# Block products in four column groups of TensorE, and the convolution's norm spread over the last two blocks of the projection

## What is computed

```python
h = rmsnorm(x, norm_mix)
z = h @ w_in                       # 256 x 6104 columns
u_glu, q_nsa, kv_nsa, g_nsa, c_q, c_kv, k_rope, g_merge = split(z)

# the convolution: 31 taps per channel, then a layer norm over 512 channels
a, b = split(u_glu); u = a * sigmoid(b)
u = depthwise_conv(u, conv_w) + conv_b
y_conv = silu(layernorm(u, ln_g, ln_b)) @ w_branch_conv

# the compressed attention's blocks: 15 overlapping windows of 32 rows, 2 groups, 64 channels
blk = tok[:, idx] + pos            # 30 rows (15 windows x 2 groups) of 32 * 64 = 2048
k_cmp = gelu(blk @ w1_k + b1_k) @ w2_k       # w1: 2048 x 256, once for keys, once for values
v_cmp = gelu(blk @ w1_v + b1_v) @ w2_v
```

## Time and profile before

| | before |
|---|---|
| median of 3 runs | 2211.2 us (2202.96 to 2211.48) |
| the profiled execution | 2208.97 us, span 2207.5 us |
| TensorE busy | 2122.1 us, 96% |
| VectorE busy | 1365.1 us, 62% |
| ScalarE busy | 1127.2 us, 51% |
| mean granted TensorE clock | 0.985 |

### The profile page before, as it was taken

One profiled execution on the slowest core, in us unless ns is written; L12 is line 12 of the kernel. 1 busy time (PEld: TensorE's weight loads), 2 busy tenths in 40 slices (PEclk: granted clock), 3 DMA queues, 4 the chain that ended last, 5 costly groups with the idle time before them and its releaser, 6 DMA issues.

```text
span 2207.5 us, 25418 instructions
## 1 busy us (share of the span) xinstructions
PE 2122.1 (96%) x9936; PEld 1736.3 (79%) x9936; DVE 1365.1 (62%) x1948; ACT 1127.2 (51%) x1818; POOL 72.0 (3%) x106
## 2 busy tenths in 40 slices
PE   8999899999999989999999999979999999999998
PEld 6877787888887778788788877658788788877887
DVE  5977655554797665555465447665655655577553
ACT  5547455443555546544454446534544544377442
POOL 0000100000000200000000000100000000010000
PEclk9999999999999999999999999989999999999999
DMA  6562353555555234345455544313555555544453
GB/s 236 193 216 89 121 181 122 189 187 177 189 191 191 80 131 154 139 184 191 172 189 184 190 181 172 129 43 115 193 181 189 190 183 189 190 177 165 178 187 133
DMA packets 52950, 369.27 MB, mean 167 GB/s; under 512 B 6207, under 2 KB 6463, under 8 KB 9312
## 3 DMA queue, kind: packets, MB, share of 16 engines
q1 hardware_dynamic: 49104, 356.54, 44.7%
q10 hardware_dynamic: 3216, 9.53, 1.4%
q0 software_dynamic: 512, 1.57, 0.4%
HBM read 366.31 MB, written 1.31 MB: 167 GB/s over the span
## 4 chain that ended last, share of the span: by engine, by line
PE 86%; DVE 6%; ACT 5%; issue 1%; DMA 0%; POOL 0%; ACTq 0%; DVEq 0%
PE ps L481 25%; PE ps L483 25%; PE ps L482 25%; PE ps L569 2%; DVE nT_lo L1243 2%; PE ps L620 1%; DVE ring_lo L1181 1%; PE ps L742 1%; PE ps L553 1%; PE ps L604 1%; ACT nT_hi L1975 1%; ACT upper_w L1911 1%; ACT ostage L1963 1%; PE ps L821 1%; PE ps L539 1%
## 5 line engine op out<-in xcount | busy, mean ns | idle before, releaser
L482 PE MATMUL ps<-ring_lo,nT_hi 128*128 128x512 f32 x1952 | 764.2, 392 | 0.0
L1181 DVE TENSOR_TENSOR ring_lo<-ring,upper_w 128x1024 fp32r<-128x1024 f32 x443 | 536.1, 1231 | 279.7 <-ACT upper_w L1911 276.9
L1911 ACT CAST upper_w<-ring 128x1024 fp32r<-128x1024 f32 x443 | 456.2, 1056 | 340.7 <-PE ps L483 170.8
L481 PE MATMUL ps<-upper_w,nT_hi 128*128 128x512 f32 (+1 forms) x1352 | 540.5, 400 | 19.0 <-DVE ring_lo L1181 11.5
L483 PE MATMUL ps<-upper_w,nT_lo 128*128 128x512 f32 (+1 forms) x1224 | 478.8, 391 | 0.0
L482 PEld LDWEIGHTS ps<-ring_lo,nT_hi 128*128 128x128 f32 x1952 | 370.9, 190 | 73.3 <-issue 0.5
L481 PEld LDWEIGHTS ps<-upper_w,nT_hi 128*128 128x128 f32 x1352 | 257.6, 191 | 78.6 <-issue 9.5
L483 PEld LDWEIGHTS ps<-upper_w,nT_lo 128*128 128x128 f32 x1224 | 232.1, 190 | 49.1
L482 PE MATMUL ps<-ring_lo,z_hi 128*128 128x512 f32 x624 | 242.9, 389 | 0.0
L483 PE MATMUL ps<-upper_w,tT_lo 128*128 128x512 f32 (+1 forms) x528 | 206.8, 392 | 0.0
L1181 DVE TENSOR_TENSOR ring_lo<-ring,PT_w 128x1024 fp32r<-128x1024 f32 x108 | 129.5, 1223 | 73.8 <-ACT PT_w L1911 73.1
(11 more groups left out here) (330 smaller groups left out, 2492.5 us busy)
## 6 DMA issues: line engine op xcount, KB each, us to landing
ring<-in_w SPq DMA_DIRECT2D x339, 1024.0 KB, 4.8
big<-in_gains ACTq DMA_DIRECT2D x7, 512.0 KB, 4.7
z<-in_mem ACTq DMA_DIRECT2D x2, 1024.0 KB, 5.1
big<-skew POOLq DMA_DIRECT2D x8, 192.0 KB, 7.0
x<-in_x SPq DMA_DIRECT2D x2, 512.0 KB, 4.9
xn<-in_w ACTq DMA_DIRECT2D x1, 1024.0 KB, 10.7
out<-x ACTq DMA_DIRECT2D x2, 512.0 KB, 2.7
const<-in_const ACTq DMA_DIRECT2D x1, 529.0 KB, 3.5
```

What stands on the lines that cost most here:

```text
L481: PE.matmul(out, hi, w_hi, start=start, stop=False)
L482: PE.matmul(out, hi, w_lo, start=False, stop=False)
L1181: V.tensor_tensor(ring_lo[:, q % RING, cols], ring[:, q % RING, cols], upper(n).bitcast(F32), ALU.subtract).then_inc(*lo_cut.up(h))
L1911: A.copy(upper(n), ring[:, q % RING, part * HALF:(part + 1) * HALF]).then_inc(*hi_cut.up(h))
```

## The change

- The stream gets the four chunks of block weights as `cmp0` to `cmp3` at other places (`CMP_AT`): one behind in3, one behind in4, two behind in5. TensorE runs eight block products at each of these places (`block_product`).
- Within eight, product j goes to the PSUM partitions that start at 32 * (j % 4). So there are four partial sums of 30 rows for keys and for values, in four groups of columns of the array, and each group starts its own sum.
- The four partial sums are added by the transposing product: its right-hand side was the unit matrix of 30, and is now `fold`, 128 x 30 with four unit matrices under one another, which VectorE makes once per layer by one reduction in in8. `hid` is copied from all 128 partitions. (The rows 30, 31 and so on of each group, which no product writes, meet zeros in `fold`.)
- The convolution's last taps, 25 to 30, stand later on VectorE, between cuts of in6; mean, centring and squares are in in6 behind the block scores instead of ahead of in6, the variance is behind in6's last half instead of its second, the deviation, root, scaling and silu follow in in6 and in7.

```diff
@@ weight_stream @@
+CMP_AT = {3: (0,), 4: (1,), 5: (2, 3)}
             w.add(f"{l}.in{b}", [at + 2 * b, at + 2 * b + 1])
+            for piece in CMP_AT.get(b, ()):
+                w.add(f"{l}.cmp{piece}", [at + 24 + piece], split=False)
...
-        w.add(f"{l}.cmp", range(at + 24, at + 28), split=False)
@@ tensor_program @@
+            def block_product(piece):
+                kind, cc = piece // 2, piece % 2
+                if piece == 0:
+                    PE.wait_ge(*dve_out.at(f"{l}.b.2"))
+                    free(6)
+                h = W.span[f"{l}.cmp{piece}"][0]
+                q = W.halves[h][0]
+                PE.wait_ge(*landed[q % RING].at(q))
+                w = ring[:, q % RING, :]
+                for j in range(8):
+                    o = 32 * (j % 4)
+                    m = PE.matmul(ps[o:o + 30, 6, kind * 256:(kind + 1) * 256], cmpb[:, kind, 8 * cc + j, :, :].rearrange("p g c -> p (g c)"),
+                                  w[:, j * 256:(j + 1) * 256], start=(cc == 0 and j < 4), stop=(cc == 1 and j >= 4))
...
+            rows_in(3, (2, 3), {0: blocks})
+            block_product(0)
+            rows_in(4, (0, 1))
+            block_product(1)
+            rows_in(5, (2, 3))
+            block_product(2)
+            block_product(3)
...
-                        m = PE.matmul(ps[:, 7, o:o + 30], hid[:, kind, ht * P:(ht + 1) * P], ident[0:30, 0:30], start=True, stop=True)
+                        m = PE.matmul(ps[:, 7, o:o + 30], hid[:, kind, ht * P:(ht + 1) * P], fold, start=True, stop=True)
...
-            rows_in(6, (0, 1), {0: hidden, 1: lambda: (block_rows(), variance()), 2: block_scores})
+            rows_in(6, (0, 1), {0: hidden, 1: block_rows, 2: lambda: (block_scores(), mean()), 3: variance})
@@ vector_program @@
+                if n == 0:
+                    V.tensor_reduce(fold, ident.rearrange("p (q i) -> p i q", q=4)[:, 0:30, :], AX_X, ALU.add).then_inc(*dve_out.up(f"{l}.fold"))
...
-            cuts(f"{l}.in5", lambda n: tap(22 + n))
-            for k in range(26, CONV_W):
-                tap(k)
-            cut_first(f"{l}.in6")
+            cuts(f"{l}.in5", lambda n: tap(22 + n) if n < 3 else None)
+            cut_first(f"{l}.in6", 1)
+            tap(25)
+            cut_first(f"{l}.in6", 2)
+            tap(26)
+            tap(27)
...
-            work = {1: lambda: (block_keys(), deviation()), 2: block_scores, 3: lambda: (scaled(), block_weights())}
-            cuts(f"{l}.in6", lambda n: work.get(n, lambda: None)())
-            cuts(f"{l}.in7", lambda n: block_values() if n == 3 else None)
+            work = {0: lambda: tap(28), 1: lambda: (block_keys(), tap(29), tap(30)), 2: lambda: (block_scores(), centre()), 3: lambda: (block_weights(), deviation())}
+            cuts(f"{l}.in6", lambda n: work[n]())
+            late = {0: scaled, 3: block_values}
+            cuts(f"{l}.in7", lambda n: late.get(n, lambda: None)())
@@ scalar_program @@
-            rows_in(5, 2, block_of(z, 3), ACT.Sigmoid)
+            cuts(f"{l}.in5")
+            cut_first(f"{l}.in6", 2)
+            A.wait_ge(*product(f"{l}.cmp3"))
+            A.copy(hid, ps[:, 6, :].rearrange("p (k n) -> p k n", k=2)).then_inc(*act_out.up(f"{l}.hid"))
+            scaled(f"{l}.in5", block_of(z, 3), ps[:, 2:4, :], func=ACT.Sigmoid)
...
-            rows_in(6, 0, block_of(z, 4), ACT.Sigmoid, {0: hidden, 1: block_rows, 2: deviation, 3: block_weights})
-            rows_in(7, 2, block_of(z, 5), ACT.Sigmoid, {1: normed, 2: weights_turned})
+            cut_to(W.halves[W.span[f"{l}.in6"][2]][2])
+            hidden()
+            rows_in(6, 0, block_of(z, 4), ACT.Sigmoid, {1: block_rows, 3: lambda: (squared(), block_weights())})
+            rows_in(7, 2, block_of(z, 5), ACT.Sigmoid, {0: deviation, 1: normed, 2: weights_turned})
```

More of the change, by code:

```diff
@@ L757, in hidden @@
                 PE.wait_ge(*act_out.at(f"{l}.hid"))
+                PE.wait_ge(*dve_out.at(f"{l}.fold"))
                 free(7)
@@ L2156, in hidden, with squared @@
                                      ).then_inc(*act_out.up(f"{l}.hidT" if kind and ht else None))
+            def squared():
+                A.wait_ge(*dve_out.at(f"{l}.centered"))
+                A.activation(sq, acc4, ACT.Square).then_inc(*act_out.up(f"{l}.sq"))
             def deviation():
```

37 lines of the change are left out of this document (8 added, 29 removed).

## The result

| | median, us | runs | lowest to highest |
|---|---|---|---|
| before | 2205.9 | 12 | 2198.4 to 2212.2 |
| after | 2194.8 | 12 | 2191.2 to 2197.1 |

The ratio is 0.9949, with a 95% interval of 0.9934 to 0.9964: the changed kernel is **11.2 us faster** (7.9 to 14.6). Forecast were 0.9972 and 2204.9 us, from 2196 to 2217. The ratio forecast lies outside the interval and the time lies 1.2 us under the range. Of the 10.1 us between forecast and time, 5.3 are not the forecast's working but its base: the three runs of before that it started from have a median of 2211.2, the twelve one of 2205.9. The rest, 6.3 us forecast against 11.2 measured, is the working.

What follows compares the result with a forecast made beforehand. Two nearly bound engines: TensorE, busy 2122 of 2207.5 us, with VectorE as full in the changed stretch. Per layer 4.1 us gained by the walk less 1.0 for the tail, twice, 6.3 us: 2204.9 us, range 2196 to 2217.

Steps and rivals of the forecast that it cites:

- Term 1: Block products on TensorE: eight take 1.96 us in column groups instead of 3.49, 6.0 us per layer if nobody waits.
- The bounds: Price of a run of eight block products: 0.87 us with four at a time, 3.49 us with no overlap.
- the forecast's own walk: Step-by-step timing of TensorE, VectorE and ScalarE from in5's end through in7, giving 4.1 us gained per layer.
- Rival 1: Block products: full overlap, 0.87 us for a run of eight; 10.7 us gained in all, 2200.5 us; chance 0.20.
- Term 2: From in5's end through in6 and in7: last tap ends at 17.8 us, in7 at 36.2; 4.1 us gained per layer.
- The 1.4 us of wait ahead of the mean: In in6: TensorE reaches the mean at 16.4 us after in5's end and waits 1.4 for the last tap.
- The 0.6 ahead of the variance: Behind in6: TensorE waits 0.6 us for ScalarE's squares before the variance.
- Term 3: Tail from in7 to conv0: later root, scaling, silu and table load delay convT and conv0, 1.0 us lost per layer.
- edits at nothing: Fold, wider copy, transposing product, chunk order (0.5 us, covered) and first run's block copies (0.1 to 0.2 us): no cost.
- Rival 4: Block products: each change of column group empties the array, 4.8 us per run, 15 us lost, 2226 us; chance 0.10.

Runs made afterwards that it cites:

- neighbours: After, with products that follow one another put in the same column group (32*(j//2) instead of 32*(j%4)); ratio 0.9950 to before, 11.0 us faster.
- two_groups: After, with two column groups instead of four, sums copied and folded from 64 partitions; ratio 0.9983 to before, 3.7 us faster; two profiles.
- early_tail: early_both, with ScalarE rounding the convolution's result ahead of in7's scaling instead of behind it; ratio 0.9914 to before, 18.9 us faster.
- after_again: The changed kernel, unchanged, profiled a second time; its two stretches from in3's turn to conv0 took 153.08 us.
- early_both: early_taps, with block copies one cut earlier in in3 and keys' copies ahead of in6's last cut; ratio 0.9923 to before, 17.0 us faster.
- groups_only: Before, with the block products in four column groups and the fold, places and order unchanged; ratio 0.9983 to before, 3.8 us faster.
- spread_only: After, with all block products in one column group, copied and turned from 30 rows without the fold; ratio 1.0032 to before, 7.1 us slower.
- before_again: The kernel before, unchanged, profiled a second time; its two stretches from in3's turn to conv0 took 163.13 us.
- early_taps: After, with two convolution taps moved on VectorE from behind in5 into in4; ratio 0.9937 to before, 13.9 us faster.

## Why the forecast missed

**Term 1 failed, in its rule.** It put a run of eight at 1.96 us and it takes 1.00. The bounds (0.87 and 3.49 us) held, the value between them was argued from "records start in program order", and that was taken from rows in which every record uses the same columns. Such rows can't show what two groups do. Measured is 1.00, near the lower bound, and neighbours shows that the order plays no part. By the forecast's own walk full overlap gives 10.7 us instead of 6.3, so this step is what parts it from the 11.2 measured. The Trainium skill, page "TensorE: Matmul & The Clock Gate", section "Measured speedup vs the span model", has 2.38 times for three column tiles; no kernel here ran three, but two gave 3.61/1.92, 1.9 times, and four 3.61/1.07, 3.4 times, so its direction agrees, and its estimate of 1.47 us was nearer than the forecast's own value. The section "The mechanism" of the same page says that matmuls start and end strictly in program order; neighbours, with its 1.09 us and the eighth record that starts fourteenth, doesn't agree with that where records of different groups meet.

**Rival 1 was the case** (chance 0.20): it gave 10.7 us, and 11.2 were measured. That they agree so closely is in part luck. In the stretches the profiled executions gain only 7.2 us (159.85 - 152.61). The slow clock, which the rival doesn't have, took 4.5 of them; without it the stretches would be at about 148.1 us by this estimate, 11.7 less than before. The 4 us between 7.2 and 11.2 lie outside the stretches or in what executions differ by.

**Term 2 held.** "VectorE keeps three taps for the end of in5 ...: 17.8": the mean started 17.7 us after in5's end in after (150.85 - 133.18) and 18.0 in two_groups. That its start hangs on a load and ScalarE's gelus, and not on the length of the products, is shown by the two having nearly the same start with runs of 1.0 and of 1.9 us. In after the third cast started at 139.02, 5.8 after in5's end (walked: 6.4), the gelus ended at 9.0 (9.4). The 1.4 us of wait ahead of the mean came as two, 1.22 at the keys and 1.26 at the tap, since with the short runs TensorE is early at both. The 0.6 ahead of the variance is there in two_groups and not in after, where TensorE itself was slow.

**Term 3** was 1.0 us and is 0.40 in layer 0 and 0.93 in layer 1 of after, 0.94 and 0.96 in two_groups: the size is right, in one layer of after it is less. Early_tail, where the wait goes when the rounding stands ahead of the scaling, shows its cause.

**Two "edits at nothing" were not.** The first run's wait for the block copies was put at 0.1 to 0.2 us and is 0.96, in after_again 1.68. In the chain that ended last it starts with a load of the ring, 5.60 us from 96.30; the cast behind it is at 101.97, the cut at 103.06, and the eight copies, with one more cut between them, end at 108.93. The chunk is late because one chunk of block weights is now ahead of it, which the forecast saw and put at 0.5 us "covered". The same cause lets VectorE stand still for 5.43 us ahead of 119.92, where before it idled 2.19. That cover was there for the taps and not for the copies, which TensorE needs at once. Together this is 1 to 1.7 us, in layer 0 alone.

**Not forecast at all: the clock.** The mean ran wholly or partly at half clock in both layers of both profiles of after. What the rows show of it: it came in six of six layers that had a wait of 1.07 us or more at the keys and another of 1.25 at the tap (after, after_again and neighbours), in none of the ten layers in the five profiles of two_groups, early_both and early_tail, where one of the two waits or both are short or gone, and now and then elsewhere (groups_only behind 6.6 us of idle time, layer 1 of spread_only behind one wait of 0.98 us, before_again, one layer in each profile of early_taps). A single wait often left it alone: 1.68 us ahead of 108.58 in after_again, 1.25 at the tap in two_groups. In layer 0 of after it had already fallen when the wait at the tap ended. That two waits close together bring it on fits this, but no run took the waits away and nothing else, so it is argued, not shown.

**Rival 4 is out**: two_groups and after change the group at every product, and the edges of a run cost 0.09 us ahead of it (133.18 to 133.27) and 0.1 behind. The page "TensorEngine Tiling (Array Packing)", section "Key Properties", of the Trainium skill says that a change of mode drains the array; if it does here, a drain is within those 0.1 us.

**Open:** the runs put after 7.5 us ahead of two_groups (0.9949 against 0.9983), the stretches only 1.5. Some 4 us of that lie in what each is set against: before took 2205.9 us beside the one and 2201.7 beside the other, at mean granted clocks of 0.987 and 0.989 (for the first, over the 29 runs made with the experiments beside it), and 0.002 of 2200 us is, as an estimate, 4.4 us. Some 2 us more lie in after's profiles, which were slower than most of its runs: 2196.9 and 2199.6 us at clocks of 0.986 and 0.985, where the twelve runs have 2194.8 and 0.988. So differences of a few us between kernels that were not run beside one another are not shown by the ratios.

## What to carry to other kernels

Where many small products like these (30 of 128 columns of the array, 256 rows streamed) follow one another, spread them over the column groups: the order within a run didn't matter here, and the run became 1.9 times shorter with two groups and 3.4 times with four. But work that leaves the bound engine is worth only what the engines that ran beside it can follow: here both halves of the change were needed. Another 6 to 8 us by the ratios (early_both and early_tail against after) came from moving VectorE's and ScalarE's steps; of the 9.3 us by early_both's first profile 4.5 are the clock, which stayed full there. Where a price has no row, check whether the rule by which you choose within the bounds comes from rows in which the new thing could have shown at all.

## What the hardware did that was not expected

- Records of products in different column groups pass each other. Eight products of 128x30 by 128x256 in 32-bit floats, two records each of 0.38 us, took 3.61 us in one group, 1.92 in two and 1.07 in four, and 1.09 in four with neighbours in the same group. In neighbours the record that stands eighth in the program starts fourteenth. The weight loads, 0.104 us each, did not line up either: in after sixteen of them lie within 0.61 us.
- After 1.94 us of work in 3 us TensorE's granted clock fell to 0.50 for some 6 us, in the middle of a kernel that keeps it busy 96% of the time. Two gaps of 1.2 us came with 2.8 us of lost work in layer 0 of after; that the gaps are the cause is argued above, not shown.
